# Six convolution groups with both parts of x in one 512-column product, and the mLSTM output gate as a sigmoid on ScalarE

## The chip, the cores and the metric

The kernel runs on one core of a Trainium2 chip. The metric is the device time of one execution in microseconds (us); lower is better. The engines of the core are TensorE (PE in the profile; PEld is its weight load), VectorE (DVE), ScalarE (ACT), GpSimd (POOL) and SyncE (SP), which starts the loads from memory. Each engine works through its own list of instructions in order and waits on semaphores that the others raise.

## The reference, cut to what matters

256 tokens of width 1024 pass through two blocks in float32. The change touches the first one. Its input projection makes, among others, the three inputs of a short convolution and the output gate of an mLSTM:

```python
h = rmsnorm(x, norm_mix_g)
proj = h @ w_in                      # [256,1024] @ [1024, N_IN]
(ml_q, ml_k, ml_v, ml_o, ml_i, ml_f, sc_b, sc_c, sc_u, sb_q, sb_k, sb_v,
 g_ml, g_sc, g_sb) = split(proj)
h_tilde = mlstm(ml_q, ml_k, ml_v, i_pre, f_pre)
y_ml = head_rmsnorm(sigmoid(ml_o) * h_tilde, ml_norm_g, ML_HEADS)
y_sc = sc_b * causal_depthwise_conv3(sc_c * sc_u, conv_w)
y_sb = stick_breaking(sb_q, sb_k, sb_v)
merged = (sigmoid(g_ml) * (y_ml @ w_ml_proj) + sigmoid(g_sc) * (y_sc @ w_sc_proj)
          + sigmoid(g_sb) * (y_sb @ w_sb_proj))
```

The rest (output projection, MLP, the whole second block) is the same in both kernels.

## The kernel before

Every large product is done in three parts. A float32 operand is split into a leading part in fp32r (`whi`, `xT_hi`) and a rest (`wlo`, `xT_lo`), and the product is leading x leading, leading x rest and rest x leading. `xT` holds both parts of x transposed, 256 columns of the leading part and 256 of the rest for each of 8 blocks of 128 rows.

The work is cut into groups of 512 output features (`GROUPS`), and each group into units of 4 blocks of 128 weight rows (`UNITS`). The groups around the change are two units long each: mlo0 (units 24, 25), mlo1 (26, 27), scc0 (28, 29), scc1 (30, 31), scu0 (32, 33), scu1 (34, 35), scb0 (36, 37), scb1 (38, 39), then gsb0 (40, 41). mlo is the mLSTM's output gate, scc, scu and scb are the convolution's inputs, gsb0 is a branch gate.

All engines run the same loop over units, each with its own part. SP loads the weights of a unit into one of three buffers `land`. ACT rounds them to `whi` (`split`, line 1077; those of unit u + 2 once PE has finished unit u - 1); DVE subtracts to get `wlo` (line 1504). Both do this as the first thing in their part of the loop. PE multiplies (`product`, lines 544 to 556). After some units PE does small products for two attentions that run alongside: `sb_remain` after unit 28, `sb_values` after units 27 and 29, `ml_scores` and `ml_values` after units 30 to 34, and the transposes `turn("yml")` after unit 38.

PSUM has eight banks of 512 columns. Four (`m`) serve the attentions, four (`acc`) the groups, two to a group, in turn: `acc[:, n % 2]`. A group in the "feat" form has four chunks of 128 features by 256 tokens, two to a bank, and each chunk takes three matmuls of 256 columns for each block of rows. With two groups' banks in turn, a group may begin once the group before the last one has been read out of its banks.

A group is read once, when its last unit is done, by one instruction of DVE over 1024 columns: scc times `row_sq` into `cT` (line 1972), scu times `cT` into `zT` (line 1979), scb times `conv` (line 1987). After scu0 and after scb0 DVE also runs `conv_taps`, twelve instructions for one half of the convolution. All this stands in DVE's list behind the weight split of the same unit. The order is written out by hand; nothing plans it.

The gate mlo is computed in two steps. ACT, in the unit behind the group's last one, takes exp(-x) (line 1380, with `minus_rstd` that GpSimd makes), and DVE in units 28 to 31 adds 1 and takes the reciprocal (`output_gate`, lines 1597 and 1598), one of four pieces in each unit. ACT's tables of functions are swapped by ACT_TABLE_LOAD.

Of the kernel before, what the change touches and what calls it, by code (L numbers as in the profile page):

```python
# [11 lines left out]
P = 128  # L12
# [160 lines left out]
GATE0 = SB0 + SB_H  # L173
# [6 lines left out]
def build(nc, dram, out):  # L180
# [26 lines left out]
    minus_rstd = sb("minus_rstd", [P, TT], side="right")  # L207
# [134 lines left out]
    half_hi, half_lo = sem("half_hi"), sem("half_lo")  # L342
    hi_ready, lo_ready, units_done = sem("hi_ready"), sem("lo_ready"), sem("units_done")
# [8 lines left out]
    half_in, ones_in, heat_set, minus_ready = (sem(n) for n in ("half_in", "ones_in", "heat_set", "minus_ready"))  # L352
# [128 lines left out]
    def _(pe):  # L481
# [36 lines left out]

        def product(u, between):
# [5 lines left out]
            if k0 == 0 and n >= 2:  # L525

                for eng, seen in (("act", read_act), ("dve", read_dve)):
                    if eng in readers(GROUPS[n - 2][0]):
                        pe.wait_ge(seen, reads_before(n - 2, eng))
                if GROUPS[n - 2][0][:3] == "mix":  # L530
                    pe.wait_ge(gained, 3 + int(GROUPS[n - 2][0][3]))
            for k in range(m):
# [7 lines left out]
                if form == "tok":  # L540
                    for t in range(TT):
                        to = acc[:, n % 2, t, 0:w]
# [4 lines left out]
                else:  # L547

                    for c in range(w // P):
                        to = acc[:, n % 2, c // 2, (c % 2) * T:(c % 2 + 1) * T]  # L550
# [8 lines left out]

        def group_read(n):  # L560

            for eng, seen in (("act", read_act), ("dve", read_dve)):
                if eng in readers(GROUPS[n][0]):
                    pe.wait_ge(seen, reads_before(n, eng))
# [66 lines left out]
        def tile_product(u, t):  # L631
# [4 lines left out]
            s, ts, to = u % PARTS, slice(t * P, (t + 1) * P), acc[:, n % 2, t, :]  # L636
# [28 lines left out]
        def first_gated(u, between):  # L665
# [5 lines left out]
            def over(k, weight, moving, opens=False, ends=False):  # L671
                for c in range(NG // P):
                    to = acc[:, n % 2, c // 2, (c % 2) * T:(c % 2 + 1) * T]
                    last = mm(to, weight[:, s, k, c * P:(c + 1) * P], moving[:, k0 + k, :],
                              start=opens and c % 2 == 0, stop=ends, skip_group_check=True)
# [328 lines left out]
        for u in range(NU):  # L1004
# [10 lines left out]
            elif whole(name):  # L1015
                whole_product(u, between)
            elif name == "gu0":
# [39 lines left out]
    def _(act):  # L1057
# [63 lines left out]
        def tile_square(name, t):  # L1121
# [8 lines left out]
            activate(tok[:, t, half * NG:(half + 1) * NG], acc[:, G_AT[name] % 2, t, :], ACT.Square,  # L1130
# [12 lines left out]
        def root_table():  # L1143

            activate(gss[:, 2, 0:1], ident[:, 0:1], ACT.Sqrt)

# [156 lines left out]
        for u in range(NU):  # L1303
# [30 lines left out]
            if u > 0 and u - 1 == LAST_U[before] and before[:2] == "gu":  # L1334
                gu_leading(before)
            if u == 0:
# [38 lines left out]
            if u - 1 in (LAST_U["mlo0"], LAST_U["mlo1"]):  # L1375
                j = int(u - 1 > LAST_U["mlo0"])
                product_done(f"mlo{j}")
                act.wait_ge(minus_ready, 1)
# [14 lines left out]
            if ends and name[:3] in ("gsb", "gml", "gsc"):  # L1393
# [3 lines left out]
                for t in range(TT):  # L1397
                    last = activate(gate[:, t], acc[:, n % 2, t], ACT.Sigmoid, scale=rstd[:, 0, t:t + 1])
                last.then_inc(read_act, 1)
            if u == TURN_ML:  # L1400
                turn_split("yml", ymlT_hi)
            if ends and name[:3] == "scb":
# [49 lines left out]
            if ends and name == "mv":  # L1452
                product_done(name)
                for t in range(TT):
                    last = activate(mbv[:, t, :], acc[:, n % 2, t, :], ACT.Copy, scale=factor3[:, t:t + 1])
# [16 lines left out]
            if ends and name[:2] == "gu":  # L1472
# [6 lines left out]
                else:  # L1479
                    activate(up2[:, j % 2], acc[:, n % 2, 1, :].rearrange("p (a b) -> p a b", b=T),  # L1480
# [6 lines left out]
    def _(dve):  # L1487
# [65 lines left out]

        def sb_softplus(h):
# [758 lines left out]
```

## Time and profile before

| | |
|---|---|
| median of 3 runs | 922.23 us (919.97 to 922.33) |
| the profiled execution's own time | 922.42 us |
| its span, first to last instruction | 920.7 us |
| mean granted TensorE clock | 0.997 |
| busy: PE, PEld, DVE, ACT, POOL | 99%, 86%, 64%, 53%, 5% |
| matmuls | 5334 |
| PE's waits for other engines, all together | seven, 7.8 us |

Matmuls overlap, so their busy time says less than the distance from one start to the next. A row of the timeline has the start in us from the span's beginning, the busy time in us, engine, line, operation, output and inputs, shape, count, and in brackets the idle time before it with what ended it. Rows of equal kind in a row are merged (x count). "Granted clock" is 1.00 at 2.4 GHz and 0.5 at 1.2 GHz.

### The profile page before, as it was taken

How to read it: one execution, taken by the hardware profiler on the slowest of the kernel's cores; microseconds unless marked ns; L12 is line 12 of the kernel's file. 1: busy time of each engine (PE TensorE's matmuls, PEld its weight loads, DVE VectorE, ACT ScalarE, POOL GpSimd, SP SyncE). 2: the span in 40 equal slices, each digit the busy share in tenths (PEclk: the TensorE clock that was granted, in tenths of full speed). 3: DMA queues.
4: the chain of work that ended last, by engine and by line, in shares of the span. 5: the costliest groups of instructions: out<-in, count | busy, mean ns of one | idle time of the engine just before them, and what ended most of it. 6: DMA issues, size and time to landing. Idle time of an engine off the chain costs nothing. (4 is left out here: it accounts for less than half of the span.)

```text
span 920.7 us, 12881 instructions
## 1 busy us (share of the span) xinstructions
PE 907.2 (99%) x5334; PEld 791.6 (86%) x5334; DVE 591.8 (64%) x614; ACT 489.7 (53%) x573; POOL 45.4 (5%) x80
## 2 busy tenths in 40 slices
PE   8999999999999999999999999999999989999997
PEld 7998998789998888888888888889987878888886
DVE  4765656567887445556677755557795767777643
ACT  6434877883435443345555543446777755555441
POOL 3010111110010000000000000001000100000000
PEclk9999999999999999999999999999999999999999
DMA  7766444544255555555565565544832475555541
GB/s 251 235 245 227 157 142 136 181 137 132 98 184 183 186 196 205 191 190 201 179 185 186 191 207 194 183 140 144 277 136 92 139 227 184 183 183 206 203 163 46
DMA packets 99818, 163.93 MB, mean 178 GB/s; under 512 B 4896, under 2 KB 37507, under 8 KB 99632
## 3 DMA queue, kind: packets, MB, share of 16 engines
q1 hardware_dynamic: 99760, 163.11, 53.8%
q8 instruction: 42, 0.69, 0.3%
q14 instruction: 16, 0.13, 0.0%
HBM read 162.03 MB, written 3.16 MB: 179 GB/s over the span
## 5 line engine op out<-in xcount | busy, mean ns | idle before, releaser
L1504 DVE TENSOR_TENSOR wlo<-land,whi 128x2048 fp32r<-128x2048 f32 (+2 forms) x152 | 335.1, 2208 | 176.8 <-ACT whi L1077 175.8
L1077 ACT ACTIVATE whi<-land 128x2048 fp32r<-128x2048 f32 (+1 forms) x152 | 280.4, 1848 | 206.8 <-PE acc L546 145.5
L552 PE MATMUL acc<-xT,whi 128*128 128x256 f32 x528 | 152.1, 288 | 0.0
L554 PE MATMUL acc<-xT,whi 128*128 128x256 f32 x528 | 149.3, 283 | 0.0
L556 PE MATMUL acc<-xT,wlo 128*128 128x256 f32 x528 | 149.3, 283 | 0.0
L552 PEld LDWEIGHTS acc<-xT,whi 128*128 128x128 f32 x528 | 101.1, 192 | 2.9 <-issue 2.1
L554 PEld LDWEIGHTS acc<-xT,whi 128*128 128x128 f32 x528 | 101.2, 192 | 0.2
L556 PEld LDWEIGHTS acc<-xT,wlo 128*128 128x128 f32 x528 | 101.2, 192 | 0.0
L544 PE MATMUL acc<-whi,xT 128*128 128x512 f32 (+2 forms) x240 | 91.5, 381 | 0.0
L545 PE MATMUL acc<-wlo,xT 128*128 128x512 f32 (+2 forms) x240 | 90.3, 376 | 0.0
L546 PE MATMUL acc<-whi,xT 128*128 128x512 f32 (+2 forms) x240 | 90.1, 375 | 0.0
L589 PE MATMUL acc<-xT,whi 128*128 128x512 f32 x288 | 70.6, 397 | 2.6 <-DVE gu L2155 2.6
L589 PE MATMUL m<-xT,whi 128*128 128x512 f32 x288 | 68.7, 391 | 0.0
L589 PEld LDWEIGHTS acc<-xT,whi 128*128 128x128 f32 x288 | 53.7, 191 | 13.4 <-DVE gu L2155 3.0
L589 PEld LDWEIGHTS m<-xT,whi 128*128 128x128 f32 x288 | 52.9, 188 | 10.3
L544 PEld LDWEIGHTS acc<-whi,xT 128*128 128x128 f32 x240 | 45.1, 188 | 9.5 <-issue 1.0
L546 PEld LDWEIGHTS acc<-whi,xT 128*128 128x128 f32 x240 | 45.1, 188 | 8.3
L545 PEld LDWEIGHTS acc<-wlo,xT 128*128 128x128 f32 x240 | 45.1, 188 | 7.6
L544 PE MATMUL acc<-whi,aT_hi 128*128 128x512 f32 x128 | 49.9, 390 | 0.0
L545 PE MATMUL acc<-wlo,aT_hi 128*128 128x512 f32 x128 | 49.8, 389 | 0.0
L546 PE MATMUL acc<-whi,aT_lo 128*128 128x512 f32 x128 | 49.8, 389 | 0.0
L594 PEld LDWEIGHTS acc<-xT,wlo 128*128 128x128 f32 x288 | 37.3, 193 | 1.5
(401 smaller groups left out, 1374.5 us busy)
## 6 DMA issues: line engine op xcount, KB each, us to landing
land<-in_w_in SPq DMA_DIRECT2D x55, 1024.0 KB, 5.1
land<-in_w_up SPq DMA_DIRECT2D x16, 1024.0 KB, 5.3
land<-in_w_down SPq DMA_DIRECT2D x16, 1024.0 KB, 5.1
land<-in_w_ffn_gate SPq DMA_DIRECT2D x22, 512.0 KB, 4.0
land<-in_w_ffn_up SPq DMA_DIRECT2D x22, 512.0 KB, 5.1
land<-in_w_ffn_down SPq DMA_DIRECT2D x10, 1024.0 KB, 5.0
land<-in_w_in SPq DMA_DIRECT2D x14, 512.0 KB, 4.6
land<-in_w_out SPq DMA_DIRECT2D x6, 1024.0 KB, 5.1
```

Of the source, the lines that this page charges most:

```text
L544: mm(to, xh[:, k0 + k, ts], whi[:, s, k, 0:w], start=first, stop=False)
L545: mm(to, xh[:, k0 + k, ts], wlo[:, s, k, 0:w], start=False, stop=False)
L546: last = mm(to, xl[:, k0 + k, ts], whi[:, s, k, 0:w], start=False, stop=end)
L552: mm(to, whi[:, s, k, cs], xh[:, k0 + k, :], start=first and c % 2 == 0, stop=False, skip_group_check=True)
L554: mm(to, whi[:, s, k, cs], xl[:, k0 + k, :], start=False, stop=False, skip_group_check=True)
L556: last = mm(to, wlo[:, s, k, cs], xh[:, k0 + k, :], start=False, stop=end, skip_group_check=True)
L589: mm(to[:, c, :], whi[:, s, k, c * P:(c + 1) * P], xT[:, k0 + k].rearrange("p a t -> p (a t)"), start=k0 + k == 0, stop=False, skip_group_ ...
L594: last = mm(to[:, c, 0:T], wlo[:, s, k, c * P:(c + 1) * P], xT_hi[:, k0 + k, :], start=False, stop=k0 + k == kk - 1, skip_group_check=True)
L1077: activate(whi[:, u % PARTS, 0:m, 0:w], land[:, u % LANDS, 0:m, 0:w], ACT.Copy).then_inc(hi_ready, 1)
L1504: v.tensor_tensor(wlo[:, u % PARTS, 0:m, 0:w], land[:, u % LANDS, 0:m, 0:w], whi[:, u % PARTS, 0:m, 0:w].bitcast(F32), ALU.subtract).then_ ...
```

## The change

The six groups scc, scu and scb take a new form, `chunk_product`. For a chunk the four blocks of rows are multiplied first by 512 columns, both parts of x side by side, then `wlo` by 256 columns. One chunk now fills a bank: columns 0 to 255 hold the sum over x's leading part, columns 256 to 511 the product with the rest. A group fills all four banks of `acc`, its first two chunks in the banks of its own side and the last two in those of the side that the group before it used. The waits follow from that: chunk c of a group waits until chunk c of the group before has been read (`chunk_read`); scc0 waits before chunk 0 for mlo0's readers and before chunk 2 for mlo1's; gsb0, in the old form, waits until chunks 0 and 1 of scb1 have been read.

To read a chunk, ACT copies its second half into `zT` or `cT` (`copy_half`), then DVE adds the first half (`take_chunk`), and the old instruction over 1024 columns follows with SBUF operands. ACT does chunks 0 and 1 of a group behind the weight split of its last unit, and 2 and 3 at the end of that unit's part; DVE likewise.

The gate mlo becomes one sigmoid on ACT in the place of the exponential. `output_gate` and `minus_rstd` go.

```diff
+        def chunk_product(u):
+            ...
+            for c in range(NG // P):
+                to, cs = acc[:, (SIDE[n] + c // 2) % 2, c % 2, :], slice(c * P, (c + 1) * P)
+                if k0 == 0 and chunked(GROUPS[n - 1][0]):
+                    pe.wait_ge(chunk_read, chunks_before(GROUPS[n - 1][0]) + c + 1)
+                elif k0 == 0 and c == 0 and n >= 2:
+                    group_read(n - 2)
+                elif k0 == 0 and c == 2:
+                    group_read(n - 1)
+                if c == 0:
+                    pe.wait_ge(hi_ready, u + 1)
+                for k in range(m):
+                    mm(to, whi[:, s, k, cs], xT[:, k0 + k].rearrange("p a t -> p (a t)"), start=k0 + k == 0, stop=False,
+                       skip_group_check=True)
+                if c == 0:
+                    pe.wait_ge(lo_ready, u + 1)
+                for k in range(m):
+                    last = mm(to[:, 0:T], wlo[:, s, k, cs], xT_hi[:, k0 + k, :], start=False, stop=k0 + k == kk - 1,
+                              skip_group_check=True)
+                if u == LAST_U[name] and c < NG // P - 1:
+                    last.then_inc(chunk_done, 1)
+            last.then_inc(units_done, 1)
...
         def product(u, between):
+            if k0 == 0 and n >= 1 and chunked(GROUPS[n - 1][0]):
+                pe.wait_ge(chunk_read, chunks_before(GROUPS[n - 1][0]) + 2)
+            elif k0 == 0 and n >= 2:
+                group_read(n - 2)
...
+        def copy_half(name, c):
+            n, j = G_AT[name], int(name[3])
+            if c < 3:
+                act.wait_ge(chunk_done, 3 * CHUNKED.index(name) + c + 1)
+            else:
+                product_done(name)
+            k = 4 * j + c
+            to = zT[:, k, CONV_K - 1:] if name[:3] == "scu" else cT[:, k, :]
+            ...
+            activate(to, acc[:, (SIDE[n] + c // 2) % 2, c % 2, T:], ACT.Copy).then_inc(chunk_half, 1)
...
-                    last = activate(mlo[:, t, j * NG:(j + 1) * NG], acc[:, G_AT[f"mlo{j}"] % 2, t], ACT.Exp,
-                                    scale=minus_rstd[:, t:t + 1])
+                    last = activate(mlo[:, t, j * NG:(j + 1) * NG], acc[:, SIDE[G_AT[f"mlo{j}"]], t], ACT.Sigmoid,
+                                    scale=rstd[:, 0, t:t + 1])
...
+        def take_chunk(name, c):
+            ...
+                dve.wait_ge(chunk_half, COPIED.index(name) * 4 + c + 1)
+                to = zT[:, k, CONV_K - 1:] if name[:3] == "scu" else cT[:, k, :]
+                v.tensor_tensor(to, src[:, 0:T], to, ALU.add).then_inc(chunk_read, 1)
...
-        def output_gate(j, t):
-            dve.wait_ge(read_act, reads_before(G_AT[f"mlo{j}"], "act"))
-            o = mlo[:, t, j * NG:(j + 1) * NG]
-            link(v.tensor_scalar(o, o, 1.0, None, ALU.add))
-            link(v.reciprocal(o, o))
...
             if ends and name[:3] == "scu":
-                product_done(name)
+                chunks_taken(name)
-                v.tensor_tensor(zT[:, 4 * j:4 * j + 4, CONV_K - 1:], flat.rearrange("p (a b) -> p a b", b=T),
-                                cT[:, 4 * j:4 * j + 4, :], ALU.mult).then_inc(read_dve, 1)
+                z = zT[:, 4 * j:4 * j + 4, CONV_K - 1:]
+                v.tensor_tensor(z, z, cT[:, 4 * j:4 * j + 4, :], ALU.mult).then_inc(read_dve, 1)
```

ACT's list in units 28 and 29, and the head of unit 30 (`mlo` is the gate, `sba` the stick-breaking weights of heads 14 and 15, `ysbT_hi` a result of that attention), before:

```order
L1077 ACTIVATE whi<-land 128x2048
L1162 ACTIVATE sbw_hi<-sbw 128x384 x2
L1380 ACT_TABLE_LOAD
L1380 ACTIVATE mlo<-acc,minus_rstd 128x512 x2
L1077 ACTIVATE whi<-land 128x2048
L1168 ACTIVATE sba<-m 128x384 x2
L1172 ACTIVATE ysbT_hi<-m 128x256
```

The same place now:

```order
L1126 ACTIVATE whi<-land 128x2048
L1224 ACTIVATE sbw_hi<-sbw 128x384 x2
L1445 ACT_TABLE_LOAD
L1445 ACTIVATE mlo<-acc,rstd 128x512 x2
L1126 ACTIVATE whi<-land 128x2048
L1207 ACTIVATE cT<-acc 128x256 x2
L1230 ACT_TABLE_LOAD
L1230 ACTIVATE sba<-m 128x384 x2
L1207 ACTIVATE cT<-acc 128x256 x2
L1234 ACTIVATE ysbT_hi<-m 128x256
```

The gate stands where it stood. Two copies of scc0's chunks and a table load have come in ahead of `sba`, two more copies behind it.

DVE's list from the end of unit 33 to that of unit 35 (`zT` is scu's group, `conv` the taps, `wlo` a weight split, `ml_den` and `mlo` the mLSTM's result), before:

```order
L1589 SCALAR_TENSOR_TENSOR mlo<-m,ml_den,mlo 128x256 x2
L1978 MEMSET zT 128x8x2
L1979 TENSOR_TENSOR zT<-acc,cT 128x4x256
L1608 TENSOR_SCALAR conv<-zT,vecs 128x256 x4
L1610 SCALAR_TENSOR_TENSOR conv<-zT,vecs,conv 128x256 x8
L1504 TENSOR_TENSOR wlo<-land,whi 128x2048
...
L1589 SCALAR_TENSOR_TENSOR mlo<-m,ml_den,mlo 128x256 x2
L1504 TENSOR_TENSOR wlo<-land,whi 128x2048
L1979 TENSOR_TENSOR zT<-acc,cT 128x4x256
```

The same place now:

```order
L1683 SCALAR_TENSOR_TENSOR mlo<-m,ml_den,mlo 128x256 x2
L1635 TENSOR_TENSOR zT<-acc,zT 128x256 x2
L2070 MEMSET zT 128x8x2
L2072 TENSOR_TENSOR zT<-zT,cT 128x4x256
L1695 TENSOR_SCALAR conv<-zT,vecs 128x256 x4
L1697 SCALAR_TENSOR_TENSOR conv<-zT,vecs,conv 128x256 x8
L1572 TENSOR_TENSOR wlo<-land,whi 128x2048
...
L1683 SCALAR_TENSOR_TENSOR mlo<-m,ml_den,mlo 128x256 x2
L1572 TENSOR_TENSOR wlo<-land,whi 128x2048
L1635 TENSOR_TENSOR zT<-acc,zT 128x256 x4
L2072 TENSOR_TENSOR zT<-zT,cT 128x4x256
```

Nothing between the two groups has left the list, and the additions that free the banks of scu1 stand behind all of it.

DVE's list from the end of unit 37 (scb0) to that of unit 39 (scb1); `ymlT_lo` belongs to the transposed mLSTM result. Before:

```order
L1987 TENSOR_TENSOR conv<-acc,conv 128x1024
L1991 TENSOR_TENSOR yscT_lo<-conv,yscT_hi 128x1024
L1608 TENSOR_SCALAR conv<-zT,vecs 128x256 x4
L1610 SCALAR_TENSOR_TENSOR conv<-zT,vecs,conv 128x256 x8
L1504 TENSOR_TENSOR wlo<-land,whi 128x2048
L1546 SCALAR_TENSOR_TENSOR ymlT_lo<-m,vecs,ymlT_hi 128x256 x8
L1504 TENSOR_TENSOR wlo<-land,whi 128x2048
L1987 TENSOR_TENSOR conv<-acc,conv 128x1024
```

Now:

```order
L1635 TENSOR_TENSOR cT<-acc,cT 128x256 x4
L2079 TENSOR_TENSOR conv<-cT,conv 128x1024
L2082 TENSOR_TENSOR yscT_lo<-conv,yscT_hi 128x1024
L1695 TENSOR_SCALAR conv<-zT,vecs 128x256 x4
L1697 SCALAR_TENSOR_TENSOR conv<-zT,vecs,conv 128x256 x8
L1572 TENSOR_TENSOR wlo<-land,whi 128x2048
L1614 SCALAR_TENSOR_TENSOR ymlT_lo<-m,vecs,ymlT_hi 128x256 x8
L1572 TENSOR_TENSOR wlo<-land,whi 128x2048
L1635 TENSOR_TENSOR cT<-acc,cT 128x256 x4
L2079 TENSOR_TENSOR conv<-cT,conv 128x1024
```

Here too the additions have come in behind the same list.

## Rows read from the trace of the kernel before

**Rows 1.** Waits of PE, whole span: who for whom, us in total, times, longest.
```profile
PE acc L589 <- DVE gu L2155: 2.6, 1, 2.6
PE acc L605 <- ACT xT L1102: 1.9, 1, 1.9
...
```

**Rows 2.** Timeline of PE: first instructions of pieces, units 28 to 40.
```profile
196.97 0.39 PE L552 MATMUL acc<-xT,whi 128*128 128x256 f32 x1
...
203.93 0.33 PE L552 MATMUL acc<-xT,whi 128*128 128x256 f32 x1
...
209.82 0.65 PE L756 MATMUL m<-sba,sbv 128*64 128x256 f32 x4
...
241.79 0.60 PE L790 MATMUL m<-mlqT,mlkT 128*128 128x256 f32 x2
...
251.78 0.47 PE L552 MATMUL acc<-xT,whi 128*128 128x256 f32 x1
...
275.00 1.91 PE L707 MATMUL m<-con,mlo 128*128 128x128 f32 x16
...
282.50 0.40 PE L544 MATMUL acc<-whi,xT 128*128 128x512 f32 x1
```

**Rows 3.** Timeline of PE: one unit of an up group, and the next one's start.
```profile
449.81 3.82 PE L589 MATMUL m<-xT,whi 128*128 128x512 f32 x16
453.46 2.08 PE L594 MATMUL m<-xT,wlo 128*128 128x256 f32 x16
455.37 3.82 PE L589 MATMUL m<-xT,whi 128*128 128x512 f32 x16
```

**Rows 4.** Timeline of ACT, units 28 and 29.
```profile
197.09 0.39 ACT L1172 ACTIVATE ysbT_hi<-m 128x256 fp32r<-128x256 f32 x1 [1.41 <-PE m L759]
...
200.12 1.28 ACT L1380 ACT_TABLE_LOAD   x1
201.41 1.27 ACT L1380 ACTIVATE mlo<-acc,minus_rstd 128x512 f32<-128x512 f32 x2
203.09 1.92 ACT L1077 ACTIVATE whi<-land 128x2048 fp32r<-128x2048 f32 x1 [0.42 <-PE acc L556]
204.92 0.85 ACT L1168 ACTIVATE sba<-m 128x384 f32<-128x384 f32 x2
```

**Rows 5.** Groups by line and form: count, busy us, mean ns of one.
```profile
L1598 DVE RECIPROCAL mlo<-mlo 128x512 f32<-128x512 f32 x4 | 13.4, 3354 | 0.1
L1398 ACT ACTIVATE gate<-acc,rstd 128x512 f32<-128x512 f32 x12 | 7.6, 686 | 18.5 <-PE acc L546 18.5
```

**Rows 6.** Timeline of POOL, unit 29.
```profile
205.51 0.89 POOL L2192 TENSOR_SCALAR_AFFINE_SELECT sba<-sba 128x256 f32<-128x256 f32 x2 [8.63 <-ACT sba L1168]
```

**Rows 7.** Timeline of DVE, units 28 to 39.
```profile
197.51 0.42 DVE L1567 TENSOR_TENSOR ysbT_lo<-m,ysbT_hi 128x256 fp32r<-128x256 f32 x1 [1.18 <-ACT ysbT_hi L1172]
...
244.92 0.56 DVE L1573 TENSOR_TENSOR sba<-m,sba 128x384 f32<-128x384 f32 x1 [3.68 <-POOL sba L2192]
...
256.87 2.28 DVE L1504 TENSOR_TENSOR wlo<-land,whi 128x2048 fp32r<-128x2048 f32 x1
259.07 1.22 DVE L1979 TENSOR_TENSOR zT<-acc,cT 128x1024 f32<-128x1024 f32 x1
...
269.43 1.22 DVE L1987 TENSOR_TENSOR conv<-acc,conv 128x1024 f32<-128x1024 f32 x1 [1.46 <-PE acc L556]
...
285.25 1.22 DVE L1987 TENSOR_TENSOR conv<-acc,conv 128x1024 f32<-128x1024 f32 x1
```

**Rows 8.** Timeline of PE: restart behind its longest wait.
```profile
743.79 3.50 PE L589 MATMUL acc<-xT,whi 128*128 128x512 f32 x8 [2.57 <-DVE gu L2155]
747.10 2.29 PE L594 MATMUL acc<-xT,wlo 128*128 128x256 f32 x16
```

**Rows 9.** Two stretches: busy us of PE, PEld, DVE, ACT, POOL; granted clock; DMA.
```profile
743.70:747.10 3.40, 3.31 (x9) 2.61 (x10) 2.98 (x4) 1.64 (x2) 0.00 (x0) 0.56 0.90 298
8.00:10.00 2.00, 0.60 (x6) 0.36 (x4) 0.69 (x1) 1.74 (x3) 0.00 (x0) 1.00 1.02 364
```

More of the change, by code:

```diff
@@ L152, in whole, with chunked, chunks_before @@
     return name[:2] == "up" or name[:2] == "gu" and name != "gu0"
+def chunked(name):
+    return name[:3] in ('scc', 'scu', 'scb')
+CHUNKED = [grp[0] for grp in GROUPS if chunked(grp[0])]
+COPIED = [_name for _name in CHUNKED if _name[:2] == "sc"]
+SIDE = [0]
+for _n in range(1, len(GROUPS)):
+    SIDE.append(SIDE[-1] if chunked(GROUPS[_n - 1][0]) else 1 - SIDE[-1])
+def chunks_before(name):
+    return 4 * CHUNKED.index(name)
 def reads_before(n, eng):
@@ L517, in wait_operand, with group_read @@
                 pe.wait_ge(mb_y, k1 - 4)
+        def group_read(n):
+            name = GROUPS[n][0]
+            if chunked(name):
+                pe.wait_ge(chunk_read, chunks_before(name) + 4)
+                return
+            for eng, seen in (("act", read_act), ("dve", read_dve)):
+                if eng in readers(name):
+                    pe.wait_ge(seen, reads_before(n, eng))
+            if name[:3] == "mix":
+                pe.wait_ge(gained, 3 + int(name[3]))
+        def chunk_product(u):
+            n, k0, m = UNITS[u]
+            name, _, _, kk, act, _ = GROUPS[n]
+            s = u % PARTS
+            wait_operand(name, act, k0 + m)
+            for c in range(NG // P):
[19 more added lines that the diff above has]
+            last.then_inc(units_done, 1)
         def product(u, between):
@@ L558, in product @@
             last.then_inc(units_done, 1)
[L560 to L564, printed above, removed]
         def whole_product(u, between):
@@ L1129, in tile_square @@
             j, half = (4 if name[:3] == "mix" else 6), int(name[-1])
-            activate(tok[:, t, half * NG:(half + 1) * NG], acc[:, G_AT[name] % 2, t, :], ACT.Square,
+            activate(tok[:, t, half * NG:(half + 1) * NG], acc[:, SIDE[G_AT[name]], t, :], ACT.Square,
                      scale=D ** -0.5 if j == 4 else dn_scale[:, t:t + 1],
@@ L1335, in _ @@
                 gu_leading(before)
+            if ends and name in COPIED:
+                for c in (0, 1):
+                    copy_half(name, c)
             if u == 0:
@@ L1397, in _ @@
                 for t in range(TT):
-                    last = activate(gate[:, t], acc[:, n % 2, t], ACT.Sigmoid, scale=rstd[:, 0, t:t + 1])
+                    last = activate(gate[:, t], acc[:, SIDE[n], t], ACT.Sigmoid, scale=rstd[:, 0, t:t + 1])
                 last.then_inc(read_act, 1)
@@ L1401, in _ @@
                 turn_split("yml", ymlT_hi)
+            if ends and name in COPIED:
+                for c in (2, 3):
+                    copy_half(name, c)
             if ends and name[:3] == "scb":
@@ L1454, in _ @@
                 for t in range(TT):
-                    last = activate(mbv[:, t, :], acc[:, n % 2, t, :], ACT.Copy, scale=factor3[:, t:t + 1])
+                    last = activate(mbv[:, t, :], acc[:, SIDE[n], t, :], ACT.Copy, scale=factor3[:, t:t + 1])
                 last.then_inc(read_act, 1)
@@ L1578, in ml_result @@
                 dve.wait_ge(floor_ready, 1)
+            if h % 2 == 0:
+                dve.wait_ge(read_act, reads_before(G_AT[f"mlo{h // 2}"], "act"))
             o = [M[2 * (h % 2) + t] for t in range(TT)]
@@ L1882, in _ @@
                 split(u + 2)
+            if ends and chunked(name):
+                for c in (0, 1):
+                    take_chunk(name, c)
             if u == 0:
@@ L2008, in _ @@
                 if name[:3] == "psb":
-                    v.tensor_tensor(m, acc[:, n % 2], gate[:], ALU.mult).then_inc(read_dve, 1)
+                    v.tensor_tensor(m, acc[:, SIDE[n]], gate[:], ALU.mult).then_inc(read_dve, 1)
                 else:
@@ L2012, in _ @@
                         for t in range(TT):
-                            last = v.scalar_tensor_tensor(out=gated[:, t], in0=acc[:, n % 2, t],
+                            last = v.scalar_tensor_tensor(out=gated[:, t], in0=acc[:, SIDE[n], t],
                                                           scalar=rstd[:, 0, t:t + 1], in1=gate[:, t], op0=ALU.mult,
@@ L2017, in _ @@
                     else:
-                        link(v.tensor_tensor(gated[:], acc[:, n % 2], gate[:], ALU.mult))
+                        link(v.tensor_tensor(gated[:], acc[:, SIDE[n]], gate[:], ALU.mult))
                     v.tensor_tensor(m, m, gated[:], ALU.add).then_inc(read_dve, 1)
@@ L2024, in _ @@
                 if name[:3] == "out":
-                    last = v.tensor_tensor(x, acc[:, n % 2], x, ALU.add)
+                    last = v.tensor_tensor(x, acc[:, SIDE[n]], x, ALU.add)
                 else:
@@ L2028, in _ @@
                     for t in range(TT):
-                        last = v.scalar_tensor_tensor(out=x[:, t, :], in0=acc[:, n % 2, t, :],
+                        last = v.scalar_tensor_tensor(out=x[:, t, :], in0=acc[:, SIDE[n], t, :],
                                                       scalar=up_scale[:, t:t + 1], in1=x[:, t, :], op0=ALU.mult,
```

80 lines of the change are left out of this document (46 added, 34 removed).

## The prediction

> **What bounds the kernel now.** I read the waits of PE first. Over the whole span PE waits seven times for another engine, and only two of the waits are over 1.5 us [rows 1]; none of them lies between 200 and 300 us, where the change is. So PE is the bound there: an instruction saved on PE shortens the kernel, a wait added on PE lengthens it, and what ACT, DVE or POOL gain is worth nothing unless PE waits for them. Second I read PE's timeline at the ends of the units concerned [rows 2], by starts, since the matmuls' busy times overlap. Third, for each new wait, I read the list of the engine that ends it [rows 4, 6, 7]: how long after PE's event it comes to the instruction that frees the bank.
>
> **PE's gain.** From the start of unit 35 to the transposes behind unit 38 lie four units without a gap: 275.00 - 251.78 = 23.22, so 5.81 us a unit [rows 2]. A unit in the new form has the same matmuls as one of an up group, 16 of 512 and 16 of 256 columns, in another order: 455.37 - 449.81 = 5.56 us [rows 3]. The gain is 0.245 a unit, for 12 units 2.9 us. Both forms stream 768 columns for a chunk and block; what goes is one matmul in three. Bounds: 2.7 (up to 0.02 lost at each switch of shape) to 3.1. A chunk's share of a unit is 1.39 us.
>
> **The wait for the gate's reader.** scc0's chunk 2 goes into the banks of mlo1. Before, scc0 needed only mlo0's. PE reaches unit 28 at 196.97 and chunk 2 two chunks later, at 199.75 [rows 2]. ACT reads mlo1 in unit 28, behind `ysbT_hi`, the weight split and `sbw_hi`, and is done at 201.41 + 1.27 = 202.68 [rows 4]. Its list up to there is unchanged, and a sigmoid costs what an exponential costs (12 sigmoids of this shape take 7.6 us, 0.63 each, the two exponentials 1.27) [rows 4, 5]. PE waits 2.9 to 3.0 us. Queued behind it on PE are the rest of unit 28, `sb_remain` and all later units. I take 3.0.
>
> **The wait for the stick-breaking weights.** ACT needs two more table loads, since a sigmoid now stands between the logarithm and the exponential `sba`: one in unit 27, covered, since ACT idles 1.41 us at the end of that unit [rows 4] and the load is 1.28; one in unit 29. There the copies of scc0's chunks 0 and 1 stand ahead of it too. Counted from the start of unit 29: chunk 1 ends at 2.8 plus 0.2 for the last matmul's tail, its copy (as `ysbT_hi`, 0.39) at 3.4, the load at 4.7, both `sba` at 5.55, and POOL's two masks 0.6 later (before: 205.51 + 0.89 = 206.40 against 204.92 + 0.85 = 205.77) at 6.2 [rows 4, 6]. PE wants them when unit 29 is over, at 5.6. Before, the same masks were ready 3.4 us ahead of PE's 209.82 [rows 2]. So PE waits 0.5 us; bounds 0.2 and 1.0.
>
> The Trainium skill, page "ScalarE: Activation LUTs", section "What ACT_TABLE_LOAD costs", puts about 1.38 us of drain on top of a load. The row shows none: the load starts at 200.12, takes 1.28, and the next instruction starts at 201.41 [rows 4]. By the page this wait would be 1.9 and the forecast 1.4 us higher; I go by the row.
>
> **The wait between scu1 and scb0.** The reciprocals that go (4 of 3.35 us, 13.4 us in all [rows 5]) stand ahead of the place that matters here: DVE idles 3.68 us before the mLSTM's product at 244.92, waiting for a chain that PE's `ml_scores` behind unit 33 starts at 241.79 [rows 2, 7]. From 241.79 DVE works through ml products, scu0, the taps, two weight splits and an mLSTM result, and is free for scu1 at 259.07, 17.3 us later [rows 7]. The change takes nothing out of this stretch and puts in scu0's chunks 2 and 3 and, at its end, scu1's chunk 0: three additions of 0.36 (start to start; busy 0.42, as `ysbT_lo` [rows 7]). scb0's chunk 0 may start 18.4 us behind the end of unit 33. PE has until then `ml_scores`, two units and `ml_values`: from 241.79 to 251.78 + 5.81 = 257.59, 15.8 us, and 0.5 less in the new form, 15.3. PE waits 3.1 us; bounds 2.7 and 3.4.
>
> **The wait between scb1 and gsb0.** Before, DVE came to scb1 at 285.25, 2.75 us after PE had gone on with gsb0 at 282.50 [rows 2, 7]. That cost nothing, as gsb0 has other banks. Now gsb0 waits for scb1's chunks 0 and 1. DVE's way starts with the end of unit 37 (275.00 - 5.81 = 269.19; DVE waits for it [rows 7]): 16.1 us to 285.25, plus 0.8 for scb0's last chunk (copy on ACT, then addition), plus 0.8 for the two additions: 17.7 us. The way holds the convolution's second half, two weight splits and `ymlT_lo`. PE's way is 282.50 - 269.19 = 13.3 us, less 0.5: 12.8. PE waits 4.8 us; bounds 4.4 and 5.2.
>
> **The other waits.** At scc0 to scc1 the additions are 3 us ahead of PE. At scc1 to scu0 and scu0 to scu1, DVE reaches chunk 2 only behind an `ml_products` and an `ml_result`; by the same counting it is 0.2 us ahead of PE's third chunk. I take 0, at most 0.5 each. The 24 copies on ACT (0.39 each) lie in its idle time elsewhere. The weight splits for units 40 and 41 stay ahead of their use.
>
> Sum of the waits: 3.0 + 0.5 + 3.1 + 4.8 = 11.4; with the gain 11.4 - 2.9 = 8.5 us slower.
>
> **The clock.** After PE's wait of 2.57 us at 743.79 eight matmuls of 512 columns take 747.10 - 743.79 = 3.3 us where eight take 1.8 at full clock [rows 3, 8], and the granted clock of that stretch is 0.56, so most of it ran at 1.2 GHz [rows 9]. The price is 1.5 us, and 0.2 in the unit's rest. After the 1.93 us wait near the start the clock stayed at 1.00 [rows 1, 9]. Three of the new waits are longer than 2.57. Whether all three bring a fall one row can't say. I take two, one of them behind the 4.8: 3.3 us; bounds 0 and 5.1.
>
> The Trainium skill, "TensorE: Matmul & The Clock Gate", section "A second HAM failure mode: psum-queue depth-cycling", says that cycling through PSUM's banks lets PE idle briefly between groups of matmuls, and that the clock falls and is won back again and again. That speaks against this change, which gives up the second set of banks; by this rule all three waits would fall, as in the fourth case below. The row at 743.79 agrees with it, the one at 8 us shows that a shorter gap need not.
>
> **The sum.** 8.5 + 3.3 = 11.8, on the profiled execution's own 922.42 (span 920.7 and 1.7 around it): 934.2. The median of the runs is 0.2 lower, so 934.0.
>
> **The rivals.**
> - Faster: the waits are hidden and PE keeps its gain, 922.23 - 2.9 = 919.3. It needs the readers ahead of PE at three places, and decides at the first: ACT would have to read mlo1 by 199.75 rather than 202.68. For it speaks only that DVE is 13 us lighter. Against it, ACT's list up to that read is unchanged, and DVE's relief lies before its 3.68 us of idle time. 3%.
> - DVE's relief shortens the two later chains by more than I see, and only the gate's wait with the short one and one fall of clock stay: 922.2 - 2.9 + 3.5 + 1.7 = 924.5. 5%.
> - The waits come as counted, without or with one fall of the clock: 930.7 or 932.4. The 1.93 us wait speaks for it. 22%.
> - All three waits bring a fall: 8.5 + 5.1, 935.8. 25%.
> - My forecast, two falls, 934.0: 45%.
>
> **How the numbers follow.** The last three cases with their bounds (the waits' together -1.4 and +2.2, the two margins of 0.2 included) hold 92%. From 929.0 to 937.5 holds a good 8 in 10. A measurement of this kernel tells 0.3% (2.8 us) from no change. Faster by more than that is a part of the first rival, 0.02; within it, the rest of the first and half of the second, 0.04; slower 0.94.
>
> **What would show it right or wrong.** In the changed profile: matmuls fall from 5334 by 192 to 5142; starts of a new unit are 5.56 us apart, 1.39 for a chunk. PE's waits list a 3 us wait for ACT's `mlo`, a 3 us and a 4.8 us wait for DVE's additions (before units 36 and 40), and about 0.5 for POOL's `sba`. The row of the granted clock has one to three falls of about 3.4 us between 200 and 300 us, each behind one of the long waits, and the eight matmuls of 512 columns behind it take 3.3 us. ACT has two more table loads. Behind gsb0 everything is as before, only 11 to 12 us later. I am wrong if the long waits are not there or are under 2 us, if other boundaries wait too, or if the units are not shorter.

## The result, and the profile after

The changed kernel takes 935.64 us (median of 4 runs, 935.27 to 935.94). In the same runs the kernel before takes 921.87 us (4 runs, 919.97 to 922.33). The ratio is 1.0151, with a 95% interval of 1.0139 to 1.0163: the change costs 13.8 us. The forecast was 934.0, range 929.0 to 937.5.

The page of the changed kernel's profiled execution (its own time 935.94) begins so:

```profile
span 934.2 us, 12565 instructions
PE 910.7 (97%) x5142; PEld 785.8 (84%) x5142; DVE 585.3 (63%) x630; ACT 500.0 (54%) x599; POOL 39.9 (4%) x79
```

There are 192 matmuls fewer, and PE is busy 97% of the span instead of 99%. The waits of PE, which answer to [rows 1], show what it does instead (engine, output and line, who it waits for, us in total, times, longest):

```profile
PE acc L597 <- DVE cT L1635: 4.6, 1, 4.6
PE acc L564 <- issue: 2.8, 1, 2.8
PE acc L564 <- ACT mlo L1445: 2.7, 1, 2.7
PE acc L636 <- DVE gu L2246: 2.6, 1, 2.6
PE acc L652 <- ACT xT L1151: 1.9, 1, 1.9
...
PE m L803 <- POOL sba L2283: 0.5, 1, 0.5
```

The 2.6 and the 1.9 are old. Four are new. PE's timeline has them in these places; the gaps in it answer to [rows 2]:

```profile
197.91 1.21 PE L564 MATMUL acc<-xT,whi 128*128 128x512 f32 x4
...
203.67 1.20 PE L564 MATMUL acc<-xT,whi 128*128 128x512 f32 x4 [2.68 <-ACT mlo L1445]
...
213.96 0.65 PE L803 MATMUL m<-sba,sbv 128*64 128x256 f32 x4 [0.48 <-POOL sba L2283]
...
263.84 2.05 PE L564 MATMUL acc<-xT,whi 128*128 128x512 f32 x4 [2.80 <-issue]
...
266.54 1.29 PE L564 MATMUL acc<-xT,whi 128*128 128x512 f32 x4
...
268.14 1.09 PE L564 MATMUL acc<-xT,whi 128*128 128x512 f32 x4
...
282.18 1.91 PE L754 MATMUL m<-con,mlo 128*128 128x128 f32 x16
...
294.33 0.80 PE L597 MATMUL acc<-whi,xT 128*128 128x512 f32 x1 [4.64 <-DVE cT L1635]
```

The wait at 263.84 is put down to "issue", that is to no event the profile shows. DVE's timeline names the cause there, and that of the wait at 294.33:

```profile
261.13 2.28 DVE L1572 TENSOR_TENSOR wlo<-land,whi 128x2048 fp32r<-128x2048 f32 x1
263.32 1.41 DVE L1635 TENSOR_TENSOR zT<-acc,zT 128x256 f32<-128x256 f32 x4
...
281.39 1.14 DVE L1695 TENSOR_SCALAR conv<-zT,vecs 128x256 f32<-128x256 f32 x4
...
291.33 2.28 DVE L1572 TENSOR_TENSOR wlo<-land,whi 128x2048 fp32r<-128x2048 f32 x1
293.53 1.41 DVE L1635 TENSOR_TENSOR cT<-acc,cT 128x256 f32<-128x256 f32 x4
```

The first of scu1's four additions starts at 263.32, right behind a weight split, and PE goes on 0.5 us later. Before gsb0 PE goes on 0.8 us after 293.53, when two additions are done.

The first wait's cause stands in ACT's timeline, which answers to [rows 4]:

```profile
202.35 1.26 ACT L1445 ACTIVATE mlo<-acc,rstd 128x512 f32<-128x512 f32 x2
...
211.11 1.28 ACT L1230 ACT_TABLE_LOAD   x1
212.40 0.87 ACT L1230 ACTIVATE sba<-m 128x384 f32<-128x384 f32 x2
```

Counted from start to start, less what the four matmuls ahead of a gap take elsewhere (0.47 us, and 0.56 where `sb_values` follows), the waits cost 2.85, 0.56, 2.97 and 4.81 us, 11.2 together.

The clock has four falls of about 3.4 us each up to 762 us, where the kernel before had one. Five stretches behind a wait (busy us of PE, PEld, DVE, ACT and POOL; granted clock; share of DMA; GB/s):

```profile
11.00:14.40 3.40, 3.40 (x17) 3.40 (x18) 2.53 (x5) 3.27 (x11) 0.23 (x1) 0.50 1.05 390
203.67:206.55 2.88, 2.88 (x16) 2.54 (x17) 0.00 (x0) 0.00 (x0) 0.00 (x0) 1.00 0.95 313
263.84:267.24 3.40, 3.40 (x11) 2.89 (x12) 3.33 (x5) 0.81 (x1) 1.35 (x1) 0.54 0.82 256
294.33:297.73 3.40, 3.40 (x8) 2.75 (x9) 2.17 (x4) 1.50 (x2) 0.00 (x0) 0.51 0.87 287
758.40:761.80 3.40, 3.40 (x14) 3.01 (x13) 2.90 (x2) 0.49 (x1) 0.00 (x0) 0.51 0.81 261
```

The last is the old one of [rows 8, 9]. Those at 263.84 and 294.33 stand behind new waits. The first costs 1.5 us: two chunks take 268.14 - 263.84 = 4.30 us, where two of the ten steady ones behind them take 2.81. The second costs 1.7: gsb0 takes 12.60 us from its first matmul to the first one behind it, where it takes 10.91 before. Behind the wait of 2.68 us the clock stayed at 1.00. The one at 11 us stands behind the old 1.9 us wait and was not there in the profiled execution of before. This execution was 0.33 us late already when that wait ended (10.85 against 10.52 us) and is 0.94 us late at the start of unit 28 (197.91 against 196.97), with none of the new waits in between.

The balance of the two profiled executions: 0.94 + 11.2 + 1.5 + 1.7 = 15.3 us lost, 934.2 - 920.7 = 13.5 us measured. What is left for the wider matmuls is a gain of about 1.8 us.

### The profile page after: what moved, and what is told of

It is laid out like the page before. It is cut to its first block and busy times, and to the rows that moved or that the text cites. A ratio compares the mean times of both kernels' runs of the same rounds, so it can differ in the third digit from the quotient of the medians.

```text
span 934.2 us, 12565 instructions
## 1 busy us (share of the span) xinstructions
PE 910.7 (97%) x5142; PEld 785.8 (84%) x5142; DVE 585.3 (63%) x630; ACT 500.0 (54%) x599; POOL 39.9 (4%) x79
## 5 line engine op out<-in xcount | busy, mean ns | idle before, releaser
L605 PE MATMUL acc<-xT,whi 128*128 128x256 f32 x336 | 96.6, 287 | 0.0
L607 PE MATMUL acc<-xT,whi 128*128 128x256 f32 x336 | 95.0, 283 | 0.0
L609 PE MATMUL acc<-xT,wlo 128*128 128x256 f32 x336 | 95.0, 283 | 0.0
L636 PE MATMUL acc<-xT,whi 128*128 128x512 f32 x288 | 70.0, 394 | 2.6 <-DVE gu L2246 2.6
L605 PEld LDWEIGHTS acc<-xT,whi 128*128 128x128 f32 x336 | 64.4, 192 | 2.3 <-issue 1.7
L607 PEld LDWEIGHTS acc<-xT,whi 128*128 128x128 f32 x336 | 64.4, 192 | 0.1
L609 PEld LDWEIGHTS acc<-xT,wlo 128*128 128x128 f32 x336 | 64.4, 192 | 0.0
L636 PEld LDWEIGHTS acc<-xT,whi 128*128 128x128 f32 x288 | 53.2, 189 | 13.3 <-DVE gu L2246 3.0
L564 PE MATMUL acc<-xT,whi 128*128 128x512 f32 x192 | 54.7, 407 | 5.5 <-issue 2.8
```

The lines of the kernel that those rows point to most:

```text
L564: mm(to, whi[:, s, k, cs], xT[:, k0 + k].rearrange("p a t -> p (a t)"), start=k0 + k == 0, stop=False, skip_group_check=True)
L605: mm(to, whi[:, s, k, cs], xh[:, k0 + k, :], start=first and c % 2 == 0, stop=False, skip_group_check=True)
L607: mm(to, whi[:, s, k, cs], xl[:, k0 + k, :], start=False, stop=False, skip_group_check=True)
L609: last = mm(to, wlo[:, s, k, cs], xh[:, k0 + k, :], start=False, stop=end, skip_group_check=True)
L636: mm(to[:, c, :], whi[:, s, k, c * P:(c + 1) * P], xT[:, k0 + k].rearrange("p a t -> p (a t)"), start=k0 + k == 0, stop=False, skip_group_ ...
```

## The experiments

All are compared with the kernel before on the same chip. The medians of before in the three sets were 922.4 (e1, e2, e3, e5), 922.15 (e4, e6, e7, e8) and 922.28 us (e9).

### Either half of the change alone

**e1_gate_only** is the kernel before with only the gate changed:

```diff
...
-  activate(mlo[...], acc[...], ACT.Exp, scale=minus_rstd[:, t:t + 1])
+  activate(mlo[...], acc[...], ACT.Sigmoid, scale=rstd[:, 0, t:t + 1])
...
-            if 0 <= u - GATE0 < 2 * TT:
-                output_gate((u - GATE0) // TT, (u - GATE0) % TT)
```

> The kernel before with only the output gate as ScalarE's sigmoid (no reciprocals on VectorE, two more table loads on ScalarE). Bank theory (the loss comes from PE waiting for readers of acc at three places, and from the clock behind the waits): no new reader of a bank, the load of unit 27 lies in 1.4 us of ScalarE's idle time and that of unit 29 in the 3.4 us by which the masks were ahead of PE, so 921.9 us, within 0.5, and the same seven waits of PE. Rival (table loads and the sigmoid cost PE time by themselves): 923 to 925 us, and a wait of PE for POOL's sba. Rival (VectorE's 13 us are worth something): under 921.

Measured: 922.14 us, ratio 0.9995 (0.9985 to 1.0005), and PE has the same seven waits. 13.4 us less work for DVE is worth nothing as long as PE doesn't wait for DVE.

**e2_chunks_only** is the changed kernel with the old exponential, addition and reciprocal.

> The changed kernel with the old gate: exponential on ScalarE, addition and reciprocal on VectorE in units 28 to 31. Bank theory: the 0.5 us wait for sba goes with the table load; the piece of the gate in unit 31, 3.8 us of VectorE, now stands ahead of scc1's chunks 2 and 3, so that PE waits about 3.5 us before chunk 2 of scu0, which it did not; the gate's reader, scu1 and scb1 waits stay at 2.9, 3.0 and 4.8. 935.6 - 0.5 + 3.5 = 938.6 us, 940.3 if the clock falls behind the new wait too. Rival (the gate's new form carries a good part of the loss): under 935 us.

Measured: 939.97 us, ratio 1.0194 (1.0179 to 1.0209), 4.3 us slower than the whole change. PE's waits:

```profile
PE acc L599 <- DVE cT L1637: 4.6, 1, 4.6
PE acc L566 <- DVE cT L1637: 3.5, 1, 3.5
PE acc L566 <- issue: 2.8, 1, 2.8
PE acc L566 <- ACT mlo L1447: 2.7, 1, 2.7
```

The three long waits of the whole change are there with the same lengths, and a fourth has come in before scu0. DVE's timeline shows why:

```profile
232.94 3.35 DVE L1694 RECIPROCAL mlo<-mlo 128x512 f32<-128x512 f32 x1
236.33 0.76 DVE L1637 TENSOR_TENSOR cT<-acc,cT 128x256 f32<-128x256 f32 x2
```

The additions that free scc1's banks stand behind a reciprocal, and PE's gap ends at 236.81. The wait for `sba` is gone, as its table stays loaded. So the whole cost comes from the chunks, and the sigmoid, worth nothing by itself, takes 4.3 us off it.

### Each wait taken away

**e3_gate_read_first** moves ACT's sigmoid over mlo1 to the head of its part in unit 28, ahead of `ysbT_hi`, the weight split and `sbw_hi` (the two stick-breaking steps next to it move ahead of the splits too):

```diff
...
+            if u == FIRST_U["scc0"]:
+                read_output_gate()
             if u - SB0 in range(4, SB_H + 3, 2):
                 sb_result(u - SB0 - 4)
...
```

> The changed kernel, but in unit 28 ScalarE reads mlo1 first, ahead of the attention's result, the leading parts and the weight split (VectorE takes its two leading-part subtractions ahead of its split too). Bank theory: mlo1 is read 2.6 us after PE has finished it, before PE comes to chunk 2 at 2.8: the wait of 2.7 for ScalarE's mlo goes, all else stays: 935.6 - 2.9 = 932.8 us. Behind that wait the changed kernel's clock did not fall, so nothing more comes back. Rival (PE would wait there for something else that comes later, the weights or the attention): 934 to 936 us and another wait near 203 us.

Measured: 931.4 us, ratio 1.01 (1.0085 to 1.0115). The 2.7 us wait is gone, the 4.6, the 2.8 and the 0.5 stay. That is 4.2 us under the changed kernel, 1.4 more than the wait and than was expected. In the two profiled executions 1.0 of it lies ahead of the change: the fall at 11 us is not in this one, and it comes to unit 28 at 196.89 instead of 197.91.

**e4_second_conv_late** moves the second half of the convolution (taps, product, split) from units 37 and 39 into unit 40, out of DVE's way to gsb0:

```diff
+            if u in (LAST_U["scb0"], LAST_U["scb1"] + 1):
+                j = int(u > LAST_U["scb0"])
+                if j == 1:
+                    dve.wait_ge(ysc_lo, 1)
+                    conv_taps(1)
...
```

> The changed kernel, but the convolution's second half (conv_taps(1), the product with scb1 and its split) is moved from the ends of units 37 and 39 into unit 40, behind the weight split. Bank theory: the 4.6 us of taps leave VectorE's way from the end of unit 37 to scb1's chunks; the way is then bound by the transposed mLSTM result, and by the same rows the wait before gsb0 falls from 4.6 to about 1.1 us. With no fall of the clock behind it, 935.6 - 3.5 - 1.6 = 930.5 us. Waits for mlo and before scb0 stay at 2.7 and 2.8. Rival (a wait of that length comes back a unit later, since VectorE has no room for the taps in unit 40): 934 to 936 us, with a new wait of PE for wlo before unit 42.

Measured: 930.21 us, ratio 1.0089 (1.0075 to 1.0102). The wait before gsb0 is 1.0 us instead of 4.6, and no fall stands behind it:

```profile
289.71 0.50 PE L597 MATMUL acc<-whi,xT 128*128 128x512 f32 x1 [1.00 <-DVE cT L1635]
```

**e5_chunks_ahead_of_split** places the copies and additions of chunks 0 and 1 ahead of the weight split on ACT and DVE, and `sba` ahead of the copies:

```diff
...
+            if ends and chunked(name):
+                for c in (0, 1):
+                    take_chunk(name, c)
             if u == LAST_U["mix0"]:
...
```

> The changed kernel, but ScalarE and VectorE take chunks 0 and 1 of a group ahead of the weight split of that unit, and in unit 29 ScalarE makes sba ahead of both. Bank theory: what stands ahead of the additions in VectorE's list is 2.2 us shorter, so the wait before scb0 falls from 3.0 to 0.8 and the wait before gsb0 from 4.8 to 2.6, the sba wait goes, the gate's reader stays at 2.9. 935.6 - 2.2 - 2.2 - 0.5 = 930.7, and 929.2 as the clock then doesn't fall before scb0. Rival (VectorE's additions are late because ScalarE's copies are, and not because of its own list): the splits being later makes it slower, over 935 us.

Measured: 929.96 us, ratio 1.0086 (1.0071 to 1.0101). Its waits:

```profile
PE acc L597 <- DVE cT L1638: 3.9, 1, 3.9
...
PE acc L564 <- issue: 0.6, 1, 0.6
```

The wait before scb0 goes from 2.8 to 0.6, that for `sba` is gone. The wait before gsb0 shrinks only to 3.9, where 2.6 was expected. DVE's timeline has the reason:

```profile
277.98 1.14 DVE L1698 TENSOR_SCALAR conv<-zT,vecs 128x256 f32<-128x256 f32 x4
...
287.92 0.74 DVE L1638 TENSOR_TENSOR cT<-acc,cT 128x256 f32<-128x256 f32 x2
288.58 2.28 DVE L1575 TENSOR_TENSOR wlo<-land,whi 128x2048 fp32r<-128x2048 f32 x1
```

The split of unit 39 now stands behind the two additions, 2.2 us won. But in unit 37 the same move put a split between chunk 1 and chunk 2 of scb0, and this split waits for ACT's. The taps start 0.7 us after the transposes of unit 38 (277.98 against 277.30) instead of 0.8 before them (281.39 against 282.18). 1.5 of the 2.2 us are given back. The fall of the clock at this place costs 2.6 us here instead of 1.7 (gsb0 takes 13.47 us), as it has begun 1.5 us before PE goes on and lasts 6.8 us.

### The wait filled, not removed

**e6_wait_filled** gives PE twelve matmuls of 512 columns to do between units 35 and 36, whose result nobody reads:

```diff
+            if u == LAST_U["scu1"]:
+                pe.wait_ge(ml_y, 3)
+                for _ in range(12):
+                    mm(M[0][:, :], xT_hi[:, 0, 0:P], xT[:, 0].rearrange("p a t -> p (a t)"), start=True, stop=True)
```

> The changed kernel with 12 more matmuls of 512 columns on TensorE between units 35 and 36, into a bank that nothing reads; they lie in the 2.8 us wait before scb0. If the clock falls because PE is idle there, no fall stands behind unit 35, the first chunk of unit 36 takes 1.4 us and not 2.7, and the time is 935.6 - 1.5 = 934.1 us although PE does more. If the fall has another cause (the new instruction form, the load), it stays, and the time is 935.6, or 2.6 more if the waits were not where I put them.

Measured: 933.64 us, ratio 1.0127 (1.0112 to 1.0143), 2.0 us faster than without them. PE's timeline there, and two stretches:

```profile
259.60 2.91 PE L1098 MATMUL m<-xT 128*128 128x512 f32 x12
262.56 1.17 PE L564 MATMUL acc<-xT,whi 128*128 128x512 f32 x4
```

```profile
262.00:280.00 18.00, 17.95 (x104) 15.44 (x103) 14.63 (x20) 7.57 (x8) 1.82 (x2) 1.00 0.58 192
291.62:296.00 4.38, 4.38 (x10) 3.47 (x11) 3.06 (x4) 2.48 (x2) 0.00 (x0) 0.50 0.76 239
```

The same 2.96 us pass at this place, but the clock stays at 1.00. So the fall is a cost of its own, beside the wait that brings it. At the untouched wait of 4.6 us before gsb0 the clock falls again, for 6.8 us, 2.2 of them still in the wait. Of the 2.0 us by the medians the missing fall accounts for 1.5. The rest is not shown to come from the filling: the falls at 11 us and behind the old 2.6 us wait, which this profiled execution lacks too, come and go between executions.

### All readers moved

**e7_all_moved** joins the three moves; the row-factor multiply of `mlo` moves from unit 36 behind the product of unit 37, the first convolution half goes into unit 36, the second into units 40 and 41, and `ymlT_lo` into unit 39.

> The change with its readers moved: mlo1 read first in unit 28, sba ahead of the copies, chunks 0 and 1 of each group ahead of the weight split, the convolution's first half in unit 36, its second in units 40 and 41, the mLSTM's norm behind scb0, its rest parts in unit 39. Bank theory: none of the four waits is left, no fall of the clock between 200 and 310 us, and what remains is the gain of the 512-column form as the changed kernel's starts show it, 1.8 us: 922.3 - 1.8 = 920.5 us, within 0.7. Rival (the waits move to other boundaries, since VectorE is too full for the form): 922.5 to 926 us. By my recorded size of the gain, 2.9, it would be 919.4.

Measured: 924.4 us, ratio 1.0025 (1.0016 to 1.0033). 11 of the 14 us are back, but it was expected under the kernel before and is slower. Its profile has three new waits. Two lie here, one where none was and one where the multiply went:

```profile
PE acc L597 <- issue: 1.9, 1, 1.9
...
PE m L754 <- DVE mlo L2107: 0.8, 1, 0.8
```

The first stands at 305.70 in PE's timeline. ACT's shows its cause:

```profile
297.83 1.06 ACT L1476 ACTIVATE yscT_hi<-conv 128x1024 fp32r<-128x1024 f32 x1 [8.34 <-DVE conv L2102]
...
301.36 5.51 ACT L1126 ACTIVATE whi<-land 128x2048 fp32r<-128x2048 f32 x3
```

The moved copy `yscT_hi` waits 8.3 us for DVE, and the branch gate and the weight splits are queued behind it. PE runs out of split weights.

The third lies 340 us on, in the second block. ACT's timeline and PE's:

```profile
637.44 1.91 ACT L1126 ACTIVATE whi<-land 128x2048 fp32r<-128x2048 f32 x1 [5.07 <-DMA land<-in_w_in]
```

```profile
644.66 0.38 PE L903 MATMUL m<-con,gv 128*16 128x128 f32 x2 [0.46 <-ACT lw L1315]
```

ACT's split waits for its weights until 637.44, 3.5 us later than before (633.96), though PE is only 1.56 us later than before. ACT's table load and eight sigmoids `lw` stand behind the split and end at 644.5, and PE waits for them.

**e8_all_moved_long_runs** is e7 with the first unit of each group written as 16 matmuls of 512 columns, then 16 of 256, so that the shape changes less often:

```diff
+            if first_unit:
+                for c in range(NG // P):
+                    ...
+                        last = mm(to[:, 0:T], wlo[:, s, k, cs], xT_hi[:, k0 + k, :], start=False, stop=False,
```

> As e7, but in the first unit of each group all 16 matmuls of 512 columns come before the 16 of 256, as in the up groups, so that the shape changes once in a unit and not seven times. If the gain was less than forecast because of the changes of shape, those six units take 5.56 us and not 5.62, and the kernel is 0.3 to 0.4 us faster than e7. If it was something else, such as the attention's matmuls between the units, they stay at 5.62 and the time at e7's.

Measured: 926.45 us, ratio 1.0046 (1.0034 to 1.0059), 2.0 us slower than e7. The sixteen matmuls of 512 columns take 3.8 us, so PE asks for the third chunk's bank 1.9 us into the unit instead of 2.8, before its reader is done. Its list has five such waits in three lines, 2.4 us in all; one of the lines:

```profile
PE acc L565 <- DVE cT L1659: 0.9, 2, 0.6
```

One of the six units, scc1's first, has no wait:

```profile
211.25 3.92 PE L565 MATMUL acc<-xT,whi 128*128 128x512 f32 x16
```

It ends at 216.93, after 5.68 us, where e9's same unit takes 5.72 (211.23 to 216.95). So fewer changes of shape do save something, 0.04 us here where 0.06 was expected, but the waits cost far more.

**e9_second_copy_later** mends e7's two waits: the multiply of `mlo` ahead of the product, and `yscT_hi` and its low part one unit later, behind the gate and a split.

```diff
-            if u in (LAST_U["scb0"], LAST_U["scb1"] + 2):
+            if u in (LAST_U["scb0"], LAST_U["scb1"] + 3):
                 j = int(u > LAST_U["scb0"])
                 ...
                 activate(yscT_hi[:, 4 * j:4 * j + 4, :], conv[:], ACT.Copy).then_inc(ysc_hi, 1)
```

> e7_all_moved again with two readers placed otherwise: the row-factor multiply of mlo stands ahead of the first convolution product on VectorE, and ScalarE's copy of the second convolution's result (with VectorE's low part) comes one unit later, behind the output gate's sigmoid and a weight split. In e7's trace TensorE waited 0.84 us for the multiply at 273.6 us and 1.91 us at 303.8 us for a weight split queued behind that copy, and from 640 us on it was a further 0.64 us late. Theory: those waits are what e7 had left, and the wider products are then worth some 1.8 us: 924.4 less 0.84 and 1.91, 921.7 us (921.0 to 922.4; 921.1 if the 0.64 us goes too), a hair under the kernel before. Rival: VectorE and ScalarE are full between 260 and 305 us, so a read that is moved on only hands its wait to the next one: 923.5 to 924.5 us, with waits of 2 to 3 us in sum elsewhere in that stretch.

Measured: 921.11 us (12 runs, 920.29 to 922.5), ratio 0.9991 (0.9983 to 1.0000) to the kernel before's 922.28. The wait that is left of the new ones, and three starts in PE's timeline:

```profile
PE acc L597 <- DVE cT L1650: 0.3, 1, 0.3
```

```profile
197.86 0.98 PE L564 MATMUL acc<-xT,whi 128*128 128x512 f32 x3
...
210.43 0.65 PE L803 MATMUL m<-sba,sbv 128*64 128x256 f32 x4
...
293.13 0.39 PE L597 MATMUL acc<-whi,ysbT_hi 128*128 128x512 f32 x1
```

At 197.86 it is 0.89 us behind the kernel before (196.97, [rows 2]), as its profiled execution has the fall at 11 us. Two units later it is 0.61 behind (210.43 against 209.82): 0.14 us a unit. The third row is the first matmul behind gsb0, and stands in the kernel before at 293.41:

```profile
293.41 0.39 PE L544 MATMUL acc<-whi,ysbT_hi 128*128 128x512 f32 x1
```

So here it is 0.28 us ahead. From unit 28 on that is 1.17 us net, with the 0.3 us wait still in it. Some of the lead is lost later: e9 is 0.14 us ahead at 337 us and 0.07 behind at 642 us. The medians are 1.2 us apart, at the edge of what a measurement of this kernel can tell. Executions with the same mean clock tell more: at 0.997 the ten of e9 took 920.66 to 921.63 us and the nine of the kernel before 922.10 to 922.73. With all readers in place the wider matmuls are a small gain; as the change stands it is a loss of 13.8 us.

## Why the prediction was right, and where it was not

- **The bound.** PE was the bound between 200 and 300 us. e1 shows it from one side (less DVE work, no gain), the new waits from the other.
- **The gate's reader.** Forecast 3.0, measured 2.68 as a wait and 2.85 by starts. e3 moved the reader; this wait went and the two other long ones stayed.
- **The stick-breaking weights.** Forecast 0.5, measured 0.48 (0.56 by starts). The table load starts at 211.11 and takes 1.28 us, and the next instruction starts at 212.40. The Trainium skill, page "ScalarE: Activation LUTs", section "What ACT_TABLE_LOAD costs", has 1.38 us of drain on top of the load; these rows show none, as those of the kernel before showed none.
- **scu1 to scb0.** Forecast 3.1, measured 2.80 (2.97 by starts). e5 took the split out of the way and left 0.6.
- **scb1 to gsb0.** Forecast 4.8, measured 4.64 (4.81). e4 took the convolution's second half out and left 1.0.
- **No other boundary waits.** Right for the change as it is. The prediction did not say that this hangs on the sigmoid: e2, without it, has a 3.5 us wait with a fall of the clock before scu0, 4.3 us in all. DVE's relief was priced at nothing; next to the chunks it is worth that.
- **The clock.** Two falls behind new waits, one of them behind the longest, as forecast, 1.5 and 1.7 us against 3.3 together. That it was these two was not derived, and e2 shows that it was partly luck: there the same 2.7 us wait did bring a fall. The other executions of after had the mean clocks 0.992, 0.994 and 0.994, where the profiled one had 0.992, so two of them may have had one fall fewer, though they took only 0.5 to 0.7 us less. e6 shows that idle PE, and not the new form, brings it. The prediction also read [rows 9] for more than they show: their second stretch, 8 to 10 us, ends before PE goes on at 10.52. The clock did stay at 1.00 there in the kernel before (1.00 from 10 to 20 us), but behind the same wait it fell in the changed kernel's profile. The Trainium skill, page "TensorE: Matmul & The Clock Gate", section "A second HAM failure mode: psum-queue depth-cycling", says that cycling through PSUM's banks makes the clock fall and come back again and again. Taken as a rule for each of the three long waits, as the prediction took it, this profile agrees for two and disagrees for one.
- **The mis-sized term: PE's gain.** Forecast 0.245 us a unit, 2.9 in all; measured 0.14 a unit at the start of e9 and about 1.8 us in all by the balance of the changed kernel (1.2 net in e9, with the 0.3 us wait). Both ends were a little off. For the old form the prediction took 23.22 / 4 = 5.81 us from four units, which holds unit 35's restart behind `ml_values`. Fifty steady matmuls of the old form take 6.00 us in the kernel before:

```profile
259.03 0.28 PE L556 MATMUL acc<-xT,wlo 128*128 128x256 f32 x1
...
265.03 0.28 PE L554 MATMUL acc<-xT,whi 128*128 128x256 f32 x1
```

  so 48 take 5.76. For the new form it took the up group's 5.56, with one change of shape in a unit. The chunk form changes it eight times, and ten chunks take 282.18 - 268.14 = 14.04 us, 5.62 a unit. The price of the changes had been seen ("up to 0.02 lost at each switch") but it went into the lower bound and not into the forecast, and there as one switch a unit: the bound of 2.7 leaves room for 0.24, where 0.02 at each of eight switches in twelve units is 1.9. 5.76 - 5.62 = 0.14 a unit, 1.7 for twelve.
- **The sum.** 8.5 + 3.3 was forecast on the profiled execution. Measured are 11.2 - 1.8 + 3.2 = 12.6, and 0.94 for what stands ahead of the change, the fall at 11 us for the most part, which the profiled execution of before happened to be without. The waits were forecast 0.2 too long and the falls 0.1 too dear, the gain 1.1 too large, and the 0.94 was not in the forecast: 1.7 us low for the profiled execution (934.2 against 935.94), 1.6 for the medians. Two small slips lie in the prediction's margins: two falls at its own 1.7 are 3.4 and not 3.3, and the upper bounds of its waits add up to 2.4 with the margin of the gain and not to 2.2. Neither would have moved the forecast by more than 0.1.

Four expectations of the experiments failed in part. e3 came out 1.4 us faster than expected, 1.0 of it from ahead of the change. e5's 2.6 us wait came as 3.9, as a split that goes behind two reads goes ahead of the two that follow. e7 was to be 1.8 us faster than the kernel before and was 2.2 slower, since a read that is moved out of one engine's way stood in the other's; e9 settled the two waits that come from that. e8 was to be 0.3 to 0.4 us faster than e7 and was 2.0 slower. The 0.6 us that e7 loses after 636 us is mostly the 0.46 us wait for `lw`. e9, whose split there waits for its weights too (635.34 instead of 633.96), loses 0.17. Why the weights land later there than in the kernel before stays open.

## What to carry to other kernels

Fewer matmuls for the same columns save only their fixed part, here 0.14 us of 5.76 for 16 out of 48. If they need banks that an earlier group still fills, list for each group the time at which its reader comes to it in its own engine's order, before the form is changed; here three readers were 3 to 5 us late. When a read is moved earlier, look at what moves behind it, and when a copy is moved later, at what is queued behind the copy. An edit that is worth nothing by itself (the sigmoid) can be what makes another affordable, so test halves both ways.

## What the runs showed of the hardware

- The clock can fall behind a short idle time of PE or not, with the same instructions around it and the same gap. Behind the 1.9 us wait that ends near 10 us it fell in the profiled executions of after and of e9 and not in the eight others that have it, before among them; behind 2.7 us at 203 us it fell in e2 and not in after, e4, e5 and e6; behind the old 2.6 us wait that ends between 743 and 762 us it fell in seven profiled executions and not in those of e5, e6, e7 and e8. Behind 2.80 us it fell in every profiled execution that has that wait (after, e2, e3, e4). Where the wait was 3.5 us (e2), 3.9 (e5) or 4.6 (after, e2, e3, e6) it fell each time.
- The spread of the kernel before goes with this. Of its 17 runs beside e9, four took 919.7 to 920.3 us at a mean clock of 0.999, eleven 921.6 to 922.7 (0.995 to 0.997), two 923.3 (0.995).
- The falls in these profiles last about 3.4 us, in which half the work is lost, 1.5 to 1.7 us. In e5 and e6 the one at gsb0 lasted 6.8 us, had begun 1.5 and 2.2 us before PE went on, and cost 2.6 and 2.2 us (gsb0 takes 13.47 and 13.14 us instead of 10.91).
- A unit of this kernel takes 5.62 us by starts with eight changes between 512 and 256 columns (the chunk form, ten steady chunks) and 5.56 with two, one of them to the next unit [rows 3], so a change of shape costs about 0.01 us.
